# A recurrence's solve on all four quarters of TensorE's array, two convolution taps moved to it, and records without use in its waits

## What is computed

```python
def rwkv7_scan(r, decay, k, v, kk, a):
    def step(S, inp):
        r_t, w_t, k_t, v_t, kk_t, a_t = inp
        sa = jnp.einsum('bhij,bhj->bhi', S, -kk_t)
        S = (S * w_t[:, :, None, :] + sa[..., None] * (kk_t * a_t)[:, :, None, :]
             + v_t[..., None] * k_t[:, :, None, :])
        return S, jnp.einsum('bhij,bhj->bhi', S, r_t)
    ...

def conformer_conv(h, pw1, pw1_b, dw, dw_b, ln_w, ln_b, pw2, pw2_b):
    u = jax.nn.glu(h @ pw1 + pw1_b, axis=-1)
    u = lax.conv_general_dilated(u, dw[:, None, :], (1,), [(CONV_WIDTH - 1, 0)], ...) + dw_b
    mean = jnp.mean(u, axis=-1, keepdims=True)
    var = jnp.mean(jnp.square(u - mean), axis=-1, keepdims=True)
    u = (u - mean) * lax.rsqrt(var + LN_EPS) * ln_w + ln_b
    return jax.nn.silu(u) @ pw2 + pw2_b
```

## Time and profile before

| what | value |
|---|---|
| median of three runs | 2382.8 us (2382.26 to 2383.48) |
| the profiled execution | 2383.32 us, span of its records 2381.4 us |
| TensorE busy | 2332.8 us (98%) |
| DVE, ACT, POOL busy | 1165.5, 909.3, 1161.8 us |
| mean granted clock of TensorE | 0.991 |
| DMA, mean | 84 GB/s |

### The profile page before, as it was taken

The page is one execution under the profiler, slowest core; times in us unless marked ns, Lnnn a source line. Parts: engine busy times, 40 slices in busy tenths (PEclk is TensorE's granted clock), DMA queues, the critical chain, the costliest instruction groups (busy, mean ns, idle before and its releaser), DMA issues.

```text
span 2381.4 us, 36665 instructions
## 1 busy us (share of the span) xinstructions
PE 2332.8 (98%) x13824; PEld 1915.8 (80%) x13824; DVE 1165.5 (49%) x1777; ACT 909.3 (38%) x1444; POOL 1161.8 (49%) x685
## 2 busy tenths in 40 slices
PE   8999999999999999999999899999999999999998
PEld 7888887888888888878877677888888887888887
DVE  5432146268634321476554445713625986731732
ACT  5332125467743322265643314212233435321222
POOL 5444444554565554445364415444444983544442
PEclk9999999999999999999999999999999999999999
DMA  4222223310033222232110003222322232322221
GB/s 163 97 97 97 97 88 110 122 53 1 20 100 101 90 97 96 97 115 82 61 46 29 29 2 104 97 91 97 97 88 91 89 106 80 97 97 88 97 97 53
DMA packets 56124, 200.07 MB, mean 84 GB/s; under 512 B 6224, under 2 KB 6480, under 8 KB 56016
## 3 DMA queue, kind: packets, MB, share of 16 engines
q1 hardware_dynamic: 54432, 195.82, 24.9%
q10 hardware_dynamic: 1584, 2.75, 0.3%
HBM read 196.45 MB, written 2.10 MB: 83 GB/s over the span
## 4 chain that ended last, share of the span: by engine, by line
PE 51%; DVE 2%; ACT 1%; issue 0%; ACTq 0%; DVEq 0%
PE ps L129 15%; PE ps L131 15%; PE ps L130 14%; PE ps L1964 1%; PE ps L1961 1%; PE ps L636 1%; PE ps L1950 1%; PE ps L651 0%; PE ps L2638 0%; PE ps L1922 0%; PE ps L2013 0%; DVE sb_M L2373 0%; DVE sb_aq L998 0%; DVE sb_ak_lo L1002 0%; PE ps L1974 0%
## 5 line engine op out<-in xcount | busy, mean ns | idle before, releaser
L110 POOL TENSOR_TENSOR sb_w_lo<-sb_w_raw,sb_w_hi 128x1024 fp32r<-128x1024 f32 (+1 forms) x361 | 887.9, 2462 | 946.4 <-ACT sb_w_hi L97 945.2
L129 PE MATMUL ps<-sb_xn_hi,sb_w_hi 128*128 128x512 f32 x1688 | 665.9, 394 | 2.3 <-DVE sb_xn_lo L171 2.3
L130 PE MATMUL ps<-sb_xn_lo,sb_w_hi 128*128 128x512 f32 x1688 | 658.2, 390 | 0.0
L131 PE MATMUL ps<-sb_xn_hi,sb_w_lo 128*128 128x512 f32 x1688 | 658.1, 390 | 0.0
L97 ACT ACTIVATE sb_w_hi<-sb_w_raw 128x1024 fp32r<-128x1024 f32 x362 | 380.1, 1056 | 489.4 <-PE ps L131 463.3
L129 PEld LDWEIGHTS ps<-sb_xn_hi,sb_w_hi 128*128 128x128 f32 x1688 | 316.6, 188 | 74.1 <-issue 5.1
L131 PEld LDWEIGHTS ps<-sb_xn_hi,sb_w_lo 128*128 128x128 f32 x1688 | 316.5, 188 | 67.6
L130 PEld LDWEIGHTS ps<-sb_xn_lo,sb_w_hi 128*128 128x128 f32 x1688 | 316.6, 188 | 66.5 <-issue 1.7
L131 PE MATMUL ps<-sb_hid_hi,sb_w_lo 128*128 128x512 f32 x864 | 344.5, 399 | 0.0
L129 PE MATMUL ps<-sb_hid_hi,sb_w_hi 128*128 128x512 f32 x864 | 339.3, 393 | 1.8 <-DVE sb_hid_lo L397 1.8
L130 PE MATMUL ps<-sb_hid_lo,sb_w_hi 128*128 128x512 f32 x864 | 340.4, 394 | 0.0
(11 more groups left out here) (439 smaller groups left out, 3037.7 us busy)
## 6 DMA issues: line engine op xcount, KB each, us to landing
sb_w_raw<-weights SPq DMA_DIRECT2D x365, 512.0 KB, 3.5
sb_stage<-x SPq DMA_DIRECT2D x4, 512.0 KB, 4.9
sb_abias<-table ACTq DMA_DIRECT2D x8, 256.0 KB, 4.0
out<-sb_out_stage SPq DMA_DIRECT2D x8, 256.0 KB, 2.9
...
```

The costliest lines, as they stand in the source:

```text
L110: pool.tensor_tensor(c.w_lo[:, slot, 0:width], c.w_raw[:, slot, 0:width], c.w_hi[:, slot, 0:width].bitcast(F32), ALU.subtract).then_inc(c. ...
L129: pe.matmul(out, hi, rhs_hi(k0 + k), start=first, stop=False)
L130: pe.matmul(out, hi, rhs_lo(k0 + k), start=False, stop=False)
L131: mm = pe.matmul(out, lo, rhs_hi(k0 + k), start=False, stop=last)
```

## The change

1. In the recurrence w, lv, d, u and z write or read the other half for the second head: `across(s, p)` is half p for s = 0 and the other for s = 1. Their results go to two banks, one for each s. E and W of the second head so lie on the other half; for this E's first value for s = 1 comes from 8 more products in lab, and A is turned by matmuls with halves of the identity in place of transpositions. e reads and writes `across(s, p)`.
2. lv is made right behind w0, and ScalarE copies it right behind `tok`, ahead of the next pair's value steps; d0 waits for the copy.
3. VectorE's first value of E is made in two parts.
4. The last channel tile of the convolution has 12 taps on TensorE in place of 10.
5. `busy(n)` makes n matmuls of 128x512 whose results nobody reads: 2 behind the sums of tile 6, 1 before the squares of tile 7, 5 before the wait for the mean, 9 behind the turned rows.
6. The first tile is normalised in two halves of 256 tokens (`NORM_STEPS`), and `conv_out_pe` makes the first three units in these steps.

```diff
+def across(s, p):
+    return HALF[p ^ s]
...
+        for b, p in ((b, p) for b in range(TT) for p in range(2)):
+            mm = pe.matmul(ps[across(1, p), 5, TT * CH + b * CH:TT * CH + b * CH + CH], w.BK[HALF[1], 2 * b + p, 0],
+                           AR[HALF[1], 0, token(b, p)], start=True, stop=True)
         done("lab", mm)
...
-                mm = pe.transpose(ps[:, TURN_BANKS[x], b * P:b * P + P], sources[x][:, b * P:b * P + P], c.ident[:])
+                if name == "turnA":
+                    pe.matmul(ps[:, TURN_BANKS[x], at(b, 0)], AR[:, 0, b * P:b * P + P], c.ident[:, HALF[0]], start=True, stop=True)
+                    for p in range(2):
+                        mm = pe.matmul(ps[across(1, p), TURN_BANKS[x], at(b, 1)], AR[:, 0, token(b, p)], c.ident[:, HALF[1]],
+                                       start=True, stop=True)
+                else:
+                    mm = pe.transpose(ps[:, TURN_BANKS[x], b * P:b * P + P], sources[x][:, b * P:b * P + P], c.ident[:])
...
-                mm = pe.matmul(ps[HALF[p], 6, group(b, s)], w.M[HALF[p], s, b, 0], w.D[HALF[p], s, b], start=True, stop=True)
+                mm = pe.matmul(ps[across(s, p), 6 + s, block(b)], w.M[HALF[p], s, b, 0], w.D[HALF[p], s, b], start=True,
+                               stop=True)
             done(f"w{lv}", mm)
             if lv == 0:
+                for b, s, p in tiles():
+                    mm = pe.matmul(ps[across(s, p), 4 + s, block(b)], w.M[HALF[p], s, b, 2], w.tok[HALF[p], 3, b, HALF[s]],
+                                   start=True, stop=True)
+                done("lv", mm)
                 tail(t, "var")
                 prepare(q, "lora_a")
...
             V(j, f"W{lv}")
+            if lv == 0:
+                A(j, "lv")
...
-                    mm = pe.matmul(ps[HALF[p], 4, group(b, s)], w.E[HALF[p], s, b], w.W[HALF[p], s, b], start=True, stop=True)
+                    mm = pe.matmul(ps[HALF[p], 5 + s, block(b)], w.E[across(s, p), s, b], w.W[across(s, p), s, b],
+                                   start=True, stop=True)
                 done(f"d{lv}", mm)
             for b, s, p in tiles():
-                mm = pe.matmul(ps[HALF[p], 5, group(b, s)], w.W[HALF[p], s, b], w.E[HALF[p], s, b], start=True, stop=True)
+                mm = pe.matmul(ps[across(s, p), 4, group(b, s)], w.W[across(s, p), s, b], w.E[across(s, p), s, b],
+                               start=True, stop=True)
             done(f"e{lv}", mm)
...
-            mm = pe.matmul(ps[HALF[p], 6, at(b, s)], w.E[HALF[p], s, b], w.tok[HALF[p], 0, b, HALF[s]], start=True, stop=True)
+            mm = pe.matmul(ps[HALF[p], 4 + s, block(b)], w.E[across(s, p), s, b], w.tok[across(s, p), 0, b, HALF[s]],
+                           start=True, stop=True)
...
-            mm = pe.matmul(ps[HALF[p], 7, at(b, s)], w.E[HALF[p], s, b], w.LV[HALF[p], b, HALF[s]], start=True, stop=True)
+            mm = pe.matmul(ps[HALF[p], 6 + s, block(b)], w.E[across(s, p), s, b], w.LV[across(s, p), b, HALF[s]], start=True,
+                           stop=True)
...
+        E(j, "lv")
+        done("lv", act.activation(heads(w.LV[:]), parity_banks(ps, 4), ACT.Copy))
         prepare(j + 1, "value")
...
-TAP_COUNT = (8, 8, 8, 8, 8, 8, 12, 10)
+TAP_COUNT = (8, 8, 8, 8, 8, 8, 12, 12)
...
+NORM_STEPS = ((0, slice(0, T // 2)), (0, slice(T // 2, T))) + tuple((k, slice(0, T)) for k in range(1, KD))
...
+    def busy(records):
+        for _ in range(records):
+            pe.matmul(c.ps[:, tap_bank(0)], v.u_hi[:, 0, 0:P], v.u_hi[:, 0, 0:T], start=True, stop=True)
...
+        if n == KD - 1:
+            busy(1)
         pe.wait_ge(v.s_vsq, n + 1)
         mm = sums(None, c.sq[:, n % 2], False, n == KD - 1)
+        if n == SUMMED:
+            busy(2)
     mm.then_inc(v.s_vstat, 1)
+    busy(5)
     pe.wait_ge(v.s_vmean, 5)
     token_values_pe(pe, c, 6, c.rstd_t)
     token_values_pe(pe, c, 7, v.mean).then_inc(v.s_vstat, 1)
+    busy(9)
...
+def conv_out_pe(pe, c, v, base):
+    for step, (k, cols) in enumerate(NORM_STEPS):
+        pe.wait_ge(v.s_vlow, step + 1)
+        for x in range(3):
+            pe.matmul(out, w_hi, v.y_hi[:, k, cols], start=step == 0, stop=False, skip_group_check=True)
+            pe.matmul(out, w_hi, v.y_lo[:, k, cols], start=False, stop=False, skip_group_check=True)
+            mm = pe.matmul(out, w_lo, v.y_hi[:, k, cols], start=False, stop=last, skip_group_check=True)
```

81 lines of the change are left out of this document (46 added, 35 removed).

## The result

The changed kernel takes **2386.7 us** (median of 22 runs, 2385.5 to 2389.5); the kernel before, in the same comparison, 2383.2. The ratio is 1.0014, with a 95% interval of 1.0008 to 1.0020: 2 to 5 us slower, where 3.0 us faster was forecast. The time lies inside the range that was given, the direction is wrong.

The account below looks back on a forecast made before the run. TensorE, busy for 98% of the span, was taken as the bound, with a level's bound moving to the chain D, w, W, d. Recurrence -1.2 and convolution -1.8 gave -3.0 us from 2382.8: 2379.8, range 2373 to 2388.

Parts of the forecast that it names:

- the level: Recurrence's solve: w and d groups fall from 0.98 to 0.51 us, e stays 0.95, a level takes 3.06 instead of 3.90.
- Rival 1: Recurrence: four-quarter groups on two shared banks get no faster and stay at 0.98 us; 2397.7 us in all, chance 0.08.
- pair 0: Recurrence's first pair of heads: -3.75 loop, -0.93 u and z, +2.25 layout, so -2.4 us.
- layout: Recurrence: turning A by products and lab's extra products add 2.25, 2.25, 1.7, 2.25 us in the four pairs.
- wait: Recurrence: ScalarE's early copy of lv delays var (L1878) by 3.0 us in pairs 1 and 2, 2.2 in pair 3.
- rival 2: Turning A costs only 0.9 us (-3.2) and the convolution keeps its clock (-4.1): -8.5, 2374.3 us; chance 0.25.
- the clock term of the recurrence: Low clock behind the waits ahead of var changes pairs 1, 2 and 3 by +0.7, +0.7, -0.6 us.
- Rival 3: Recurrence: the clock falls more often; four more low stretches at some 1.7 us cost 7, giving 2386.8 us; chance 0.13.
- the 0.93 of u and z: Recurrence, each pair: quicker u and z groups save 0.93 us, with what follows them still covered by the fill.
- the sum for the convolution: Convolution's end: taps +1.4 us against gains in sums, transpositions and first three units; between -4.1 and -0.45, taken as -1.8.
- I take the middle: Convolution's end: -1.8 us, between a clock kept up (-4.1) and one that falls all the same (-0.45).
- The 1.25 us: Convolution's end: normalising the first tile in halves brings the first product 1.25 us nearer.

Follow-up runs that it names:

- best2: best1 with A turned by the four transpositions of before, then eight products for the heads that change place; 2369.4 us, ratio 0.9944.
- rec_only: The kernel before with the recurrence's part of the change alone; 2385.8 us, ratio 1.0004.
- rec_records: rec_only with six 128x256 products whose result nobody reads in TensorE's wait ahead of var, in pairs 1 to 3; 2377.7 us, ratio 0.9975.
- rec_lvlate: rec_only with ScalarE's copy of lv behind the preparation's square root (root), ahead of yroot; 2376.8 us, ratio 0.9965.
- best1: The changed kernel with lv's copy behind root and VectorE's bias additions ahead of its wait for the token sums; 2372.8 us, ratio 0.9965.

## Why the prediction was wrong

**Right: the level.** TensorE's timeline of the changed kernel, the same level as the earlier trace rows:

```profile
1218.27 0.69 PE L1986 MATMUL ps<-sb_W,sb_E 64*64 64x64 f32 x32
1218.78 1.10 PE L1990 MATMUL ps<-sb_E,sb_W 64*64 64x64 f32 x32
1219.77 0.69 PE L1968 MATMUL ps<-sb_D,sb_M 64*64 64x64 f32 x32
1220.39 0.50 PE L129 MATMUL ps<-sb_xn_hi,sb_w_hi 128*128 128x512 f32 x1
...
1221.29 0.69 PE L1986 MATMUL ps<-sb_W,sb_E 64*64 64x64 f32 x32
```

w and d take 0.51 to 0.62 to the next work, e still 0.99, and the period is 3.02 us (3.06 forecast). Rival 1 is out: four quarters write two shared banks at 0.51 us a group, the rate of the earlier trace rows, and the rule of the Trainium skill that was weighed there (TensorEngine Tiling (Array Packing), "Gotcha 1: PSUM Pressure") does not show in this trace. First d to u in pair 0 is 14.67 us, 4.16 less (3.75 forecast).

**Right: layout and wait.** Turning A takes 2.41 us (2.2 forecast), lab's second part 0.47 as forecast (no run reached rival 2's price of 0.9; with other code, best2, it is 1.15). The layout as a whole moves w of level 0 by 2.3, 2.5, 1.6 and 1.7 us in the four pairs (2.25, 2.25, 1.7, 2.25 forecast). Rival 2's sum had a slip: 0.9 less in each of four pairs is -3.6, not -3.2. Var comes 5.25 us behind w in pairs 1 and 2, exactly as worked out, with the root as its releaser.

**Wrong: the clock term of the recurrence,** "+0.7, +0.7, -0.6". The forecast took 2.3, 2.3 and 2.8 us lost at the low clock. The changed trace loses 5.1 in pair 1, 6.8 in pair 2 and 6.8 from the end of pair 2 through pair 3, 18.7 in all against 10.2 before; rec_only loses 17.0, the eight traces of the old recurrence 8.5 to 13.6. rec_records shows that half of rec_only's loss is worth 7 us. The step read one trace, took its low stretches for fixed ones and let waits nearly four times as long add 0.7 us each in pairs 1 and 2. Pair by pair, the mean of the two traces of the new code against the mean of the eight of the old gives -1.5, +0.3, +3.9 and -0.5 us (forecast -2.4, +1.3, +1.2, -1.2): it is pair 2 that the sum missed. Its wait (+3.1), its loop (-3.3) and its layout (+1.6) are as forecast, and what is left, +2.5, stands where "+0.7" for the clock and "-0.93" for u and z were put. How much of the extra low clock the longer wait made is open: rec_lvlate, with short waits, still loses 15.3, best1, with the same recurrence, 10.2.

Rival 3 named this mechanism and gave it 0.13; "four more" low stretches at 1.7 was its price, and the trace has five more. That its 2386.8 is the measured time is luck: it left the convolution at -1.8, and half of the loss is the convolution's.

**Wrong, small: pair 0,** -1.5 for -2.4. z is quicker but what follows it is not: from u to the next pair's first product 22.65 us against 22.30, so the 0.93 of u and z and 0.35 more are given back: 0.75 in the products between z and the scan, where TensorE stands idle for 0.66 us and the profile shows no releaser, and 0.5 ahead of the scan's first step, which waits 0.79 us for VectorE (0.27 before). In pair 1 the 0.93 is kept (22.4 against 23.3).

**Wrong: the sum for the convolution stopped at the third unit.** Up to there it holds to a tenth in the changed kernel's trace: -3.2 us and +1.4 for the taps, -1.8. That is in part luck, as five other traces of the same code give -1.6 and +1.4, -0.2. What the prediction did not ask is who else must be early for the fifth unit. VectorE's layer end was not moved by the change, and its hand-over stood 0.8 us from being the bound. The wait (1.9 us) and what is lost around it give +2.1 for the stage, in place of -1.8. That this wait is the step that failed is shown by moving the additions: the stage falls by 2.3 us, and to 588.0 and 588.1 where the clock falls late, 1.6 us under before and so close to the -1.8 that was forecast.

Within the sum, "I take the middle" lay between a kept clock (-4.1) and one that falls among the sums (-0.45), and it fell in every trace; -1.8 is met only where it fell late. The 1.25 us by which the halves bring the first product nearer stand in neither of the two sums; the runs give 1.4 for the halves without records and nothing with them.

Together: 2.4 + 2.1 = +4.5 by the stages, +3.5 by the medians, for -3.0 forecast.
